# Gated MLP stage of a larger program: another order of block splits, products and weight loads, and two transfers moved from SyncE's queue to GpSimd's

## The chip, the cores and the metric

The program runs on 1 core of one Trainium2 chip. The time is device microseconds of one launch. Three runs of the kernel before took 3770.35, 3770.53 and 3778.82 us, the median is 3770.53 us. The change touches the first of the program's stages alone, the gated MLP mixer, which fills roughly the first 745 us; everything behind it (dilated attention, the second model's mixers, its MLP) is the same code.

## The reference

What the stage computes, with one batch, 1024 tokens, a model width of 1024, 16 heads of 128 features and chunks of 128 tokens:

```
x = residual, h = rms_norm(x, norm_pre[0])
z = h @ w_in                      # 1024 -> 3 x 2048
u, v, g = split(z, 3)
u = gelu(u);  v = layer_norm(gelu(v), vn_g, vn_b)
sg[c, p, head, d] = sum_q w_s[head, p, q] * v[c, q, head, d] + b_s[head, p]
y = u * sg * silu(g)
x = x + rms_norm(y @ w_out, norm_post[0])
```

All of it is float32. The other two mixers and the second MLP of the reference follow on the result x.

## The kernel before, in words

**Precision.** A float32 product is made of three TensorE products: each operand is split into a rounded upper part (ScalarE copies it into a `hi` tile) and a remainder (VectorE subtracts into a `lo` tile), and hi x hi, lo x hi and hi x lo are added up in PSUM. So every operand needs a ScalarE instruction and then a VectorE instruction before TensorE can use it.

**Three parts of the stage.** First the v part: 20 units (`v_units`, five passes of four) multiply h by the weights of v; after each pass ScalarE applies GELU into the staging tile `vst` (two halves, by the feature block f) and VectorE takes `bn_stats` of it; ScalarE's queue stores it to DRAM (`vhat`). Second the heads: for each of 16 heads j, u and g are computed together as a 2x2 block product with seven block products instead of eight (a Winograd form: `Pairs.BLOCKS` are sums of quarters of the weights, `PRODUCTS` names the seven blocks of h they meet: b11, t2, t3, b21, t1, t4, b22, where t1 to t4 are sums of quarters made in place in x by `combine`). Each product is 12 matmuls of 128x512. Then `gating(j)` multiplies the normalised v of that head with w_s (9 float32 matmuls, lines 700 and 702). Third the output: for two token halves and eight column blocks (`outs`), y is multiplied by w_out: `out` with 24 + 24 matmuls (line 740), weights in two buffers `w.raw[0]` and `w.raw[1]`, the lower eight k-tiles from buffer 0 and the upper eight from buffer 1.

**What sets the order.** All queues are written out by hand. Each engine runs its own function in `gmlp`; semaphores tie them. On ScalarE `block_hi(name)` and on VectorE `block_lo(name)` make a block's upper and lower tile (two instructions each), `pairs.split_hi` and `pairs.split_lo` do the same for the seven weight blocks of a head, with four slots. `add_second`, `add_lower`, `add_three`, `add_four` form the weight sums. TensorE waits before product i of a head for `lo_done`, in head 0 also for `s_blo` (the block) and `s_gelu` (the bank is free), and for what VectorE and ScalarE must have read from the bank: `s_c21` before i = 2, `s_x11` before i = 3, `s_c12` before i = 4, `s_n` before i = 5, `s_c22` before i = 6. VectorE's `difference` and the sum into n3 (line 937), and the two sums into `tg` (lines 954 and 960) combine the banks; `gates`, `swish`, `times_value` and `result` make y. The y of the first token half stays in SBUF (`y_of["raw"]`); that of the second half goes to DRAM (`y_rows`) and comes back as `y_late`.

**Tiles that share bytes.** b11 and t2 lie where the early output splits will be; t3 and b21 lie over the upper part of h, t1 and t4 over its lower part, so those four can be written only when the v part no longer reads what is under them. `vst` half 0 shares bytes with gu, tg, th and sv, half 1 with b22. `y_late` and later the residual x again (`x_kept`) lie over the lower part of h.

**Queues.** SyncE's queue issues the weight loads (`w.load` line 132, `pairs.load` lines 230 and 231), v, w_s and b_s of a head (`load_head`, lines 392 to 395), the stores of y (lines 434, 443), the loads of `y_late` (line 449) and one load of 4 MB that brings x back (line 456). GpSimd's queue (lines 1003 to 1016) makes the attention bias tables. Each waits in its written order.

Of the kernel before, what the change touches and what calls it, by code (L numbers as in the profile page):

```python
# [21 lines left out]
P = 128  # L22
# [257 lines left out]
def gmlp(nc, a, w, hi, lo, x_kept, inv, vhat, y_dram, vecs, tiles, ident, ones, yo, norms, blocks, y_of, over_w):  # L280
# [8 lines left out]
    with Stage(nc, "ag") as st:  # L289
# [45 lines left out]
        s_late, s_yhi, s_ylo = (st.sem(n) for n in ("late_in", "yhi_s", "ylo_s"))  # L335
# [18 lines left out]
        made = ("b11", "t2", "t3", "b21", "t1", "t4", "b22")  # L354
# [25 lines left out]
        def _(sp):  # L380
# [82 lines left out]
        def _(act):  # L463
# [45 lines left out]
            for u in range(3, NV):  # L509
# [51 lines left out]
            def y_upper(n):  # L561
# [5 lines left out]
                else:  # L567
                    act.wait_ge(s_late, 16 * (k // 4) + 16)
# [7 lines left out]
            block_hi("t3")  # L576
            for j in range(H):
                last = j == H - 1
                pairs.split_hi(act, j, 3)
                if j == 0:  # L580
                    block_hi("b21")
                    first_product(j)
                    nc.scalar.preload_act_table_set(SQRT_SET)
                    act.wait_ge(s_mv, 1)
                    nc.scalar.activation(sd[:, :], mv[:, :, 1:2].rearrange("p m a -> p (m a)"), ACT.Sqrt, bias=eps[:, :]).then_inc(s_sd, 1)
                    nc.scalar.preload_act_table_set(GELU_SET)
                    block_hi("t1")
                else:
                    value_late(j - 1)
# [3078 lines left out]
```

## Time and profile before

| | us |
|---|---|
| median of 3 runs | 3770.53 |
| profiled execution, its own time | 3774.28 |
| its span, first to last instruction | 3772.7 |
| TensorE busy | 3606.6 (96%) |
| VectorE busy | 1972.8 (52%) |
| ScalarE busy | 1313.0 (35%) |
| mean granted TensorE clock | 0.974 of full speed |

TensorE is busy 96% of the span, so time is lost or won where it stands still or runs at the lower clock. A row of the timeline gives start, duration, engine, line, operation, tiles, count, and in brackets the idle time just ahead and who ended it. Neighbouring instructions overlap at their ends: two 0.69 us operations on VectorE take 1.29 us together.

### The profile page before, as it was taken

The page shows a single profiled execution, that of the slowest core. Times are in us where ns is not written, and L with a number is a line of the kernel's source. Part 1 is how long each engine was busy: PE and PEld are TensorE (multiplying, and loading weights), DVE is VectorE, ACT ScalarE, POOL GpSimd, SP SyncE. Part 2 cuts the span into 40 slices and gives each one's busy share as a digit, 9 for nine tenths or more (in the row PEclk, how much of TensorE's full clock was granted, in tenths as well). Part 3 has the DMA queues.
Part 4 walks back from the last instruction along what each step waited for, and adds up shares of the span by engine and source line. Part 5 has one row for each costly group of instructions (what it writes and reads, how often), then busy time and mean ns, then how long its engine had stood idle before and what let it go on. Part 6 is the DMA issues. An engine that isn't in the chain of part 4 may idle for free. (4 is left out here: it accounts for less than half of the span.)

```text
span 3772.7 us, 48650 instructions
## 1 busy us (share of the span) xinstructions
PE 3606.6 (96%) x18034; PEld 2917.4 (77%) x18034; DVE 1972.8 (52%) x3847; ACT 1313.0 (35%) x2559; POOL 112.2 (3%) x137
## 2 busy tenths in 40 slices
PE   8999999989999999999998899999978999999999
PEld 6878877767777777777777687677977877887887
DVE  5377773263333455555555544544675567654443
ACT  3254443232323333332332434444323323233222
POOL 0000001000000000000000110000000000000000
PEclk9999999999999999999999999999988999999999
DMA  4222335321111111211111330111322322233333
GB/s 146 90 100 85 104 110 164 134 93 59 58 53 52 60 58 61 59 54 46 46 45 50 115 110 19 48 43 63 103 89 95 105 78 84 75 113 95 95 97 121
DMA packets 140772, 308.87 MB, mean 82 GB/s; under 512 B 31824, under 2 KB 70272, under 8 KB 140464
## 3 DMA queue, kind: packets, MB, share of 16 engines
q1 hardware_dynamic: 123792, 264.81, 21.6%
q0 software_dynamic: 14688, 33.22, 2.9%
q10 hardware_dynamic: 2112, 8.39, 0.6%
q8 instruction: 119, 1.95, 0.2%
q14 instruction: 61, 0.50, 0.0%
HBM read 256.55 MB, written 56.04 MB: 83 GB/s over the span
## 5 line engine op out<-in xcount | busy, mean ns | idle before, releaser
L142 DVE TENSOR_TENSOR all_w_lo<-all_w_raw,all_w_hi 128x1024 fp32r<-128x1024 f32 x295 | 361.2, 1225 | 353.5 <-ACT all_w_hi L137 353.3
L137 ACT ACTIVATE all_w_hi<-all_w_raw 128x1024 fp32r<-128x1024 f32 x295 | 310.3, 1053 | 499.2 <-PE om_z L155 261.4
L1433 PE MATMUL da_z<-all_hi,all_w_hi 128*128 128x512 f32 x736 | 306.3, 416 | 4.1 <-DVE all_w_lo L142 4.1
L1433 PE MATMUL da_z<-all_hi,all_w_lo 128*128 128x512 f32 x736 | 291.6, 396 | 0.0
L1433 PE MATMUL da_z<-all_lo,all_w_hi 128*128 128x512 f32 x736 | 290.0, 394 | 0.0
L1294 ACT ACTIVATE da_pt<-da_tr 128x512 f32<-128x512 f32 (+1 forms) x192 | 101.0, 526 | 486.0 <-PE da_tr L1486 486.0
L155 PE MATMUL om_z<-all_hi,all_w_hi 128*128 128x512 f32 x640 | 258.4, 404 | 7.4 <-DVE all_w_lo L142 4.3
L1302 ACT ACTIVATE at_p<-at_logit,da_pair_max 128x256 f32<-128x256 f32 (+1 forms) x384 | 177.9, 465 | 239.6 <-DVE da_pair_max L1688 239.2
L155 PE MATMUL om_z<-all_hi,all_w_lo 128*128 128x512 f32 x640 | 256.3, 401 | 0.0
L155 PE MATMUL om_z<-all_lo,all_w_hi 128*128 128x512 f32 x640 | 254.6, 398 | 0.0
L155 PE MATMUL pr_g<-all_hi,all_w_hi 128*128 128x344 f32 (+1 forms) x624 | 212.7, 341 | 10.6 <-issue 4.9
L155 PE MATMUL pr_g<-all_hi,all_w_lo 128*128 128x344 f32 (+1 forms) x624 | 204.2, 327 | 0.0
L155 PE MATMUL om_z<-om_h_hi,all_w_hi 128*128 128x512 f32 x512 | 202.4, 395 | 1.7 <-DVE all_w_lo L142 1.7
L155 PE MATMUL pr_g<-all_lo,all_w_hi 128*128 128x344 f32 (+1 forms) x624 | 203.2, 326 | 0.0
L155 PE MATMUL om_z<-om_h_hi,all_w_lo 128*128 128x512 f32 x512 | 200.1, 391 | 0.0
L155 PE MATMUL om_z<-om_h_lo,all_w_hi 128*128 128x512 f32 x512 | 200.1, 391 | 0.0
L1688 DVE CUSTOM_DVE_ANT_0 at_logit<-da_qk,at_bias 128x256 f32<-128x256 f32 (+1 forms) x384 | 129.9, 375 | 119.2 <-issue 115.4
L1433 PEld LDWEIGHTS da_z<-all_hi,all_w_hi 128*128 128x128 f32 x736 | 139.0, 189 | 42.0 <-issue 10.6
L1497 PE MATMUL da_pv<-at_v,da_pt 128*128 128x64 f32 x1280 | 164.0, 267 | 0.0
L1433 PEld LDWEIGHTS da_z<-all_lo,all_w_hi 128*128 128x128 f32 x736 | 138.9, 189 | 31.6
L1497 PEld LDWEIGHTS da_pv<-at_v,da_pt 128*128 128x128 f32 x1280 | 159.8, 192 | 2.1
L1433 PEld LDWEIGHTS da_z<-all_hi,all_w_lo 128*128 128x128 f32 x736 | 139.3, 189 | 25.0
(692 smaller groups left out, 7808.5 us busy)
## 6 DMA issues: line engine op xcount, KB each, us to landing
all_w_raw<-in_w_mlp SPq DMA_DIRECT2D x128, 512.0 KB, 3.5
all_w_raw<-in_w_ug SPq DMA_DIRECT2D x48, 512.0 KB, 3.9
all_w_raw<-in_w_qkv SPq DMA_DIRECT2D x48, 512.0 KB, 3.6
all_w_raw<-in_w_in SPq DMA_DIRECT2D x27, 512.0 KB, 3.5
da_w_raw<-in_w_qkv SPq DMA_DIRECT2D x24, 512.0 KB, 3.6
all_w_raw<-in_w_bo SPq DMA_DIRECT2D x24, 512.0 KB, 3.4
all_w_raw<-in_w_v SPq DMA_DIRECT2D x20, 512.0 KB, 4.7
vhat<-ag_vst ACTq DMA_DIRECT2D x4, 2048.0 KB, 7.4
```

Of the source, the lines that this page charges most:

```text
L137: self.nc.scalar.activation(self.hi[b][:, :], self.raw[b][:, :], ACT.Copy).then_inc(self.hi_done[b], 1)
L142: self.nc.vector.tensor_tensor(self.lo[b][:, :], self.raw[b][:, :], self.hi[b][:, :].bitcast(F32), ALU.subtract).then_inc(self.lo_done[b], 1)
L155: last = self.nc.tensor.matmul(out, wp[b][:, w], ap[:, k, cols], start=(k == 0 and m == 0), stop=(k == KT - 1 and m == 2))
L1294: nc.scalar.activation(pt[t % 2][:, 0:wd], tr[t % 2][:, 0:wd], ACT.Copy).then_inc(s_pt, 1)
L1302: last = nc.scalar.activation(p[t % 2][:, hh, 0:wd], logit[t % 2][:, hh, 0:wd], ACT.Exp, scale=-1.0, bias=pair_max[:, t, hh:hh + 1], accum ...
L1433: last = nc.tensor.matmul(z[h][:, :], wp[u][:, ws], ap[:, kk, cols], start=(kk == 0 and m == 0), stop=(kk == KT - 1 and m == 2))
L1497: last = nc.tensor.matmul(pv[t % 2][:, 64 * hh:64 * hh + 64], pt[t % 2][:, i * P:i * P + P], v[:, t + x, 64 * hh:64 * hh + 64], start=(x = ...
L1688: last = nc.vector.tensor_tensor_reduce(out=logit[t % 2][:, hh, 0:wd], in0=qk[hh][:, 0:wd], in1=bias[ag][hh][x][:, :], scale=1.0, scalar=3 ...
```

## The change

Six edits, all in `gmlp`:

1. The tiles change places: b22 now shares bytes with `vst` half 0, gu to sv with half 1. b22 is split already in unit 17 of the v part.
2. The blocks t3, b21 and t1 are split on ScalarE, and t3 and t1 on VectorE, in unit 19, ahead of the GELUs of the last pass; t4 and b21's lower part right after. The sums t1 and t4 are formed there too.
3. VectorE's `bn_stats` of the last pass, and the mean and variance behind it, stand after the products' first sums in head 0, and head 0's weight split 6 and its `tg` sum (`gate_late`) behind them.
4. `gating(j)` stands behind the first product of head j + 1 instead of behind the last of head j.
5. On SyncE's queue the first two pairs of output weights are issued ahead of the head 15 loads, the next two ahead of the last y store; the `y_late` loads leave that queue.
6. GpSimd's queue issues the four `y_late` loads (a semaphore each) and, after the bias tables, x in eight transfers of 512 KB. The y splits 9 to 12 come one output block later.

```diff
         with Stage(nc, "al") as late:
+            blocks["b22"] = tuple(late.sb(f"b22_{part}", [P, KT // 2, HALF], F32R) for part in ("hi", "lo"))
             gu, tg, th, sv = (late.sb(n, [P, T]) for n in ("gu", "tg", "th", "sv"))
-            blocks["b22"] = tuple(late.sb(f"b22_{part}", [P, KT // 2, HALF], F32R) for part in ("hi", "lo"))
...
-        made = ("b11", "t2", "t3", "b21", "t1", "t4", "b22")
+        made_hi = ("b11", "t2", "b22", "t3", "b21", "t1", "t4")
+        made_lo = ("b11", "t2", "b22", "t3", "t1", "b21", "t4")
...
+            def store_y(j):
+                sp.wait_ge(s_y, j + 1)
+                sp.dma_start(y_dram[j], th[:, second_half]).then_inc(s_yout, 16)
+
             for j in range(H):
                 if j == 7:
                     for b in range(2):
                         sp.wait_ge(s_vst[b], 32)
+                if j == H - 1:
+                    sp.wait_ge(pairs.lo_done, Pairs.N * (H - 1))
+                    for b in range(2):
+                        load_out(b, 0)
                 if j:
                     load_head(j)
-                    sp.wait_ge(s_y, j)
-                    sp.dma_start(y_dram[j - 1], th[:, second_half]).then_inc(s_yout, 16)
+                    store_y(j - 1)
                 if j + 2 < H:
                     load_pair(j + 2)
-            sp.wait_ge(pairs.lo_done, Pairs.N * (H - 1))
             for b in range(2):
-                load_out(b, 0)
-            for g in range(4):
-                if g == 3:
-                    sp.wait_ge(s_y, H)
-                    sp.dma_start(y_dram[H - 1], th[:, second_half]).then_inc(s_yout, 16)
-                sp.wait_ge(s_yout, 16 * (4 * g + 4))
-                if g == 0:
-                    sp.wait_ge(pairs.multiplied, Pairs.N * (H - 1) + 6)
-                if g == 3:
-                    load_out(0, 1)
-                sp.dma_start(y_of["late"][:, 4 * g:4 * g + 4, :], y_dram[4 * g:4 * g + 4].rearrange("j p t -> p j t")).then_inc(s_late, 16)
-            load_out(1, 1)
+                load_out(b, 1)
+            store_y(H - 1)
             for n in range(2, NO):
                 for b in range(2):
                     load_out(b, n)
-                if n == KT + 1:
-                    sp.wait_ge(s_ylo, len(splits))
-                    sp.dma_start(x_kept[:, :, :], a["x"]).then_inc(s_xin, 16)
             for b in range(2):
                 w.load(sp, b, n_all, a["w_qkv"][b])
-            sp.wait_ge(s_xin, 16)
+            sp.wait_ge(s_xin, 16 * KT)
             sp.wait_ge(s_norms, 16 * len(norms))
...
+                    if name == "b22":
+                        act.wait_ge(s_vst[0], 32)
+                        act.wait_ge(s_bn, 8 * 3)
...
+                if u == 17:
+                    block_hi("b22")
                 if u == NV - 1:
-                    for i in range(3):
-                        pairs.split_hi(act, 0, i)
+                    pairs.split_hi(act, 0, 0)
+                    w.left(act, 0, v_pairs)
+                    block_hi("t3")
+                    pairs.split_hi(act, 0, 1)
+                    pairs.split_hi(act, 0, 2)
+                    block_hi("b21")
+                    block_hi("t1")
+                    pairs.split_hi(act, 0, 3)
                 if u % 4 == 3:
                     geluses(v_units[u][3])
...
                 if j == 0:
-                    act.wait_ge(s_vst[0], 32)
+                    act.wait_ge(s_vst[1], 32)
+                    act.wait_ge(s_bn, 8 * 4)
...
+            block_hi("t4")
+            first_product(0)
+            for i in range(4, 7):
+                pairs.split_hi(act, 0, i)
+            value(0)
+            nc.scalar.preload_act_table_set(SQRT_SET)
+            act.wait_ge(s_mv, 1)
+            nc.scalar.activation(sd[:, :], mv[:, :, 1:2].rearrange("p m a -> p (m a)"), ACT.Sqrt, bias=eps[:, :]).then_inc(s_sd, 1)
+            nc.scalar.preload_act_table_set(GELU_SET)
+            pairs.split_hi(act, 1, 0)
+            act.wait_ge(s_shift, 1)
+            normalise(0)
+            for i in range(1, 3):
+                pairs.split_hi(act, 1, i)
...
                     last.then_inc(pairs.multiplied, 1)
-                gating(j)
+                    if i == 0 and j:
+                        gating(j - 1)
+            gating(H - 1)
...
+                if u == 17:
+                    block_lo("b22")
                 if u == NV - 1:
                     w.left(dve, 0, v_pairs)
                     pairs.add_second(dve, 0)
                     pairs.add_lower(dve, 0)
                     pairs.split_lo(dve, 0, 0)
+                    block_lo("t3")
                     pairs.add_three(dve, 0)
                     pairs.split_lo(dve, 0, 1)
+                    dve.wait_ge(s_sums, 4)
+                    dve.wait_ge(s_blo, 8)
+                    combine("t1", "t2", "b22", ALU.subtract)
                     pairs.split_lo(dve, 0, 2)
-                if u % 4 == 3:
+                    block_lo("t1")
+                    dve.wait_ge(s_sums, 6)
+                    combine("t4", "t2", "b21", ALU.subtract)
+                    pairs.split_lo(dve, 0, 3)
+                    pairs.add_four(dve, 0)
+                elif u % 4 == 3:
                     statistics(v_units[u][3])
-            block_lo("t3")
-            dve.wait_ge(s_bn, 8 * 4)
-            for m in range(KT):
-                last = nc.vector.bn_aggr(mv[:, m, :], stats[:, 4 * m:4 * m + 4, :])
-            last.then_inc(s_mv, 1)
+            w.left(dve, 1, v_pairs)
+            block_lo("b21")
...
+            pairs.split_lo(dve, 0, 4)
+            block_lo("t4")
+            difference(0)
+            pairs.split_lo(dve, 0, 5)
+            sum_of_three(0)
+            statistics(len(passes) - 1)
+            dve.wait_ge(s_bn, 8 * 4)
+            for m in range(KT):
+                last = nc.vector.bn_aggr(mv[:, m, :], stats[:, 4 * m:4 * m + 4, :])
+            last.then_inc(s_mv, 1)
+            pairs.split_lo(dve, 0, 6)
+            dve.wait_ge(s_vst[1], 32)
+            gate_late(0)
+            dve.wait_ge(s_sd, 1)
+            nc.vector.reciprocal(rstd[:, :], sd[:, :]).then_inc(s_rstd, 1)
+            dve.wait_ge(s_rstd, 1)
+            nc.vector.scalar_tensor_tensor(shift[:, :], mv[:, :, 0:1].rearrange("p m a -> p (m a)"), -1.0,
+                                           rstd[:, :], ALU.mult, ALU.mult).then_inc(s_shift, 1)
+            pairs.add_second(dve, 1)
+            pairs.add_lower(dve, 1)
+            pairs.split_lo(dve, 1, 0)
+            gate_early(0)
+            pairs.add_three(dve, 1)
+            pairs.split_lo(dve, 1, 1)
+            pairs.split_lo(dve, 1, 2)
...
+            pool.wait_ge(pairs.multiplied, Pairs.N * (H - 1) + 6)
+            for g in range(4):
+                pool.wait_ge(s_yout, 16 * (4 * g + 4))
+                pool.dma_start(y_of["late"][:, 4 * g:4 * g + 4, :], y_dram[4 * g:4 * g + 4].rearrange("j p t -> p j t")).then_inc(s_late[g], 16)
             pool.dma_start(hot, a["hot"]).then_inc(s_bin_v, 16)
...
             pool.wait_ge(s_bout, 48 + 16 * 12)
+            pool.wait_ge(s_ylo, len(splits))
+            for k in range(KT):
+                pool.dma_start(x_kept[:, k, :], a["x"][:, k, :]).then_inc(s_xin, 16)
```

How rows stand now. VectorE, from head 0's weight split 3 on (`p_lo` is the lower part of a weight block in one of four slots; ba, bb, al are where a block's tiles lie; `all_yo` is x; `all_inv` is n2 or n3). Before:

```order
L267 TENSOR_TENSOR ag_p_lo3<-all_w_raw0,ag_p_hi3 128x512 [waits ag_p_hi_done,ag_lnp_in]
L251 TENSOR_TENSOR all_w_raw0<-all_w_raw0 128x512 [waits ag_p_summed]
L805 TENSOR_TENSOR ba_b21_lo<-all_yo,ba_b21_hi 128x1024 [waits ag_block_hi] x2
L879 TENSOR_TENSOR all_inv<-all_inv,ag_bank1 128x512 [waits ag_x11_s,ag_p_multiplied]
L810 TENSOR_TENSOR all_yo<-all_yo 128x2x512 [waits ag_block_lo,ag_sums_s]
L810 TENSOR_TENSOR all_yo<-all_yo 128x2x512
L805 TENSOR_TENSOR bb_t1_lo<-all_yo,bb_t1_hi 128x1024 [waits ag_block_hi] x2
L810 TENSOR_TENSOR all_yo<-all_yo 128x2x512 [waits ag_sums_s]
L810 TENSOR_TENSOR all_yo<-all_yo 128x2x512
L267 TENSOR_TENSOR ag_p_lo0<-ow_spare,ag_p_hi0 128x512 [waits ag_p_hi_done]
```

The same engine now, from head 0's weight split 3 to the sum that TensorE needs before product 6:

```order
L267 TENSOR_TENSOR ag_p_lo3<-all_w_raw0,ag_p_hi3 128x512 [waits ag_p_hi_done]
L251 TENSOR_TENSOR all_w_raw0<-all_w_raw0 128x512 [waits ag_p_summed]
L808 TENSOR_TENSOR ba_b21_lo<-all_yo,ba_b21_hi 128x1024 [waits ag_block_hi,all_w_multiplied1]
L808 TENSOR_TENSOR ba_b21_lo<-all_yo,ba_b21_hi 128x1024 [waits ag_block_hi]
L267 TENSOR_TENSOR ag_p_lo0<-ow_spare,ag_p_hi0 128x512 [waits ag_p_hi_done,ag_lnp_in]
L808 TENSOR_TENSOR bb_t4_lo<-all_yo,bb_t4_hi 128x1024 [waits ag_block_hi] x2
L890 TENSOR_TENSOR all_inv<-all_inv,ag_bank1 128x512 [waits ag_x11_s,ag_p_multiplied]
L267 TENSOR_TENSOR ag_p_lo1<-all_w_raw1,ag_p_hi1 128x512 [waits ag_p_hi_done]
L920 TENSOR_TENSOR all_inv<-ag_bank2,all_inv 128x512 [waits ag_n_s,ag_p_multiplied]
L799 BN_STATS ag_stats<-ag_vst 128x6 [waits ag_gelu_s] x8
L939 BN_AGGR ag_mv<-ag_stats 128x2 [waits ag_bn_s]
```

The two `combine` sums and t1's lower part, which stood in this piece, are now ahead of it; the eight `bn_stats` and the `bn_aggr`, which stood ahead of it, are now in it, and weight split 6 (`ag_p_lo2`) and the sum `al_tg` come after them.

SyncE's queue from the loads of head 15 on (`ow_v`, `all_ident` and `ag_bs` are v, w_s and b_s of the head; `all_w_raw` the output weights). Before:

```order
L392 DMA ow_v<-vhat 128x1024 [waits ag_sg_s]
L393 DMA all_ident<-in_ws_t 128x128
L395 DMA ag_bs<-in_b_s 128x128 [waits ag_s_read]
L434 DMA y_rows<-al_th 128x512 [waits ag_y_s]
L132 DMA all_w_raw0<-in_w_ug 128x1024 [waits all_w_lo_done0,ag_p_lo_done]
L132 DMA all_w_raw1<-in_w_ug 128x1024 [waits all_w_lo_done1]
L449 DMA y_late<-y_rows 128x4x512 [waits ag_p_multiplied,ag_y_stored]
L449 DMA y_late<-y_rows 128x4x512 [waits ag_y_stored] x2
L443 DMA y_rows<-al_th 128x512 [waits ag_y_s]
L132 DMA all_w_raw0<-in_w_ug 128x1024 [waits all_w_lo_done0,ag_y_stored]
```

The same queue now:

```order
L132 DMA all_w_raw0<-in_w_ug 128x1024 [waits all_w_lo_done0,ag_p_lo_done]
L132 DMA all_w_raw1<-in_w_ug 128x1024 [waits all_w_lo_done1]
L394 DMA ow_v<-vhat 128x1024 [waits ag_sg_s]
L395 DMA all_ident<-in_ws_t 128x128
L397 DMA ag_bs<-in_b_s 128x128 [waits ag_s_read]
L431 DMA y_rows<-al_th 128x512 [waits ag_y_s]
L132 DMA all_w_raw0<-in_w_ug 128x1024 [waits all_w_lo_done0]
L132 DMA all_w_raw1<-in_w_ug 128x1024 [waits all_w_lo_done1]
L431 DMA y_rows<-al_th 128x512 [waits ag_y_s]
```

The first output weights no longer stand behind a store of y, the second pair no longer behind the last store and the `y_late` transfers.

## Rows read from the trace of the kernel before

**Rows 1.** Who TensorE waited for, 535 to 600 us: total, times, longest

```profile
PE ag_bank L740 <- issue: 8.0, 2, 5.3
```

**Rows 2.** The same view, 650 to 760 us

```profile
PE ag_bank L740 <- issue: 3.7, 1, 3.7
```

**Rows 3.** TensorE's timeline, head 0 to the start of head 1

```profile
198.92 0.39 PE L275 MATMUL ag_bank<-ag_b_hi,ag_p_hi 128*128 128x512 f32 x1
...
209.79 0.39 PE L275 MATMUL ag_bank<-ba_b_lo,ag_p_hi 128*128 128x512 f32 x1
217.48 0.80 PE L275 MATMUL ag_bank<-bb_t_hi,ag_p_hi 128*128 128x512 f32 x1 [7.30 <-DVE ag_p_lo L267]
...
223.52 0.39 PE L275 MATMUL ag_bank<-bb_t_lo,ag_p_hi 128*128 128x512 f32 x1
...
227.91 0.47 PE L275 MATMUL ag_bank<-al_b_hi,ag_p_hi 128*128 128x512 f32 x1 [1.95 <-issue]
...
232.68 0.48 PE L275 MATMUL ag_bank<-ag_b_hi,ag_p_hi 128*128 128x512 f32 x1
```

**Rows 4.** ScalarE's timeline: the last pass's first two GELUs, one block's upper part

```profile
194.44 1.29 ACT L485 ACTIVATE ag_vst<-ag_bank,ag_inv_col 128x512 f32<-128x512 f32 x2 [2.60 <-PE ag_bank L680]
...
200.31 2.01 ACT L495 ACTIVATE ba_t_hi<-all_yo 128x1024 fp32r<-128x1024 f32 x2 [0.50 <-ACT ag_vst L485]
```

**Rows 5.** VectorE's timeline: weight sum, statistics, one block's lower part

```profile
188.16 0.69 DVE L236 TENSOR_TENSOR ow_spare<-all_w_raw 128x512 f32<-128x512 f32 x1 [8.79 <-PE ag_bank L680]
...
195.16 1.29 DVE L796 BATCH_NORM_STATS2 ag_stats<-ag_vst 128x6 f32<-128x512 f32 x2 [2.51 <-ACT ag_vst L485]
...
201.40 2.36 DVE L805 TENSOR_TENSOR ba_t_lo<-all_yo,ba_t_hi 128x1024 fp32r<-128x1024 f32 x2 [0.86 <-ACT ba_t_hi L495]
203.68 1.11 DVE L858 BATCH_NORM_AGGREGATE ag_mv<-ag_stats 128x2 f32<-128x24 f32 x8
```

**Rows 6.** TensorE's timeline, the first two output blocks

```profile
552.53 0.47 PE L740 MATMUL ag_bank<-ye_hi,all_w_hi 128*128 128x512 f32 x1 [2.73 <-issue]
...
568.28 0.77 PE L740 MATMUL ag_bank<-ye_hi,all_w_hi 128*128 128x512 f32 x1 [5.31 <-issue]
...
578.75 0.80 PE L740 MATMUL ag_bank<-ym_hi,all_w_hi 128*128 128x512 f32 x1 [2.53 <-DVE all_w_lo L142]
...
581.86 0.39 PE L740 MATMUL ag_bank<-ym_hi,all_w_lo 128*128 128x512 f32 x1
```

**Rows 7.** VectorE's timeline and SyncE's queue, the same stretch

```profile
546.37 3.49 DVE L904 TENSOR_TENSOR ym_lo<-y_raw,ym_hi 128x1024 fp32r<-128x1024 f32 x3
551.20 1.23 DVE L142 TENSOR_TENSOR all_w_lo<-all_w_raw,all_w_hi 128x1024 fp32r<-128x1024 f32 x1 [1.35 <-ACT all_w_hi L137]
...
560.22 0.33 SPq L443 DMA_DIRECT2D y_rows<-al_th  x1
562.21 0.35 SPq L132 DMA_DIRECT2D all_w_raw<-in_w_ug  x1
```

**Rows 8.** SyncE's queue and ScalarE around the load of x

```profile
634.20 0.33 SPq L132 DMA_DIRECT2D all_w_raw<-in_w_ug  x1
656.57 0.67 SPq L456 DMA_DIRECT2D x_kept<-in_x  x1
661.40 0.34 SPq L132 DMA_DIRECT2D all_w_raw<-in_w_ug  x1
...
643.25 1.06 ACT L137 ACTIVATE all_w_hi<-all_w_raw 128x1024 fp32r<-128x1024 f32 x1 [4.96 <-DMA all_w_raw<-in_w_ug]
678.13 1.06 ACT L137 ACTIVATE all_w_hi<-all_w_raw 128x1024 fp32r<-128x1024 f32 x1 [9.71 <-DMA all_w_raw<-in_w_ug]
```

**Rows 9.** Landing of the 16 loads of v; head 3's sum ahead of product 6

```profile
DMA to landing us min/median/max: 3.1/3.3/4.3
289.76 0.69 DVE L954 TENSOR_TENSOR al_tg<-ag_bank,all_inv 128x512 f32<-128x512 f32 x1
291.23 0.39 PE L275 MATMUL ag_bank<-al_b_hi,ag_p_hi 128*128 128x512 f32 x1
```

More of the change, by code:

```diff
@@ L334, in gmlp @@
         s_x11, s_n, s_c11, s_c12, s_c21, s_c22, s_gu = (st.sem(n) for n in ("x11_s", "n_s", "c11_s", "c12_s", "c21_s", "c22_s", "gu_s"))
-        s_late, s_yhi, s_ylo = (st.sem(n) for n in ("late_in", "yhi_s", "ylo_s"))
+        s_late = st.sems("late_in", 4)
+        s_yhi, s_ylo = (st.sem(n) for n in ("yhi_s", "ylo_s"))
         block = st.block()
@@ L575, in _ @@
             w.left(act, 1, v_pairs)
-            block_hi("t3")
-            for j in range(H):
+            block_hi("t4")
[12 more added lines that the diff above has]
+                pairs.split_hi(act, 1, i)
+            for j in range(1, H):
                 last = j == H - 1
                 pairs.split_hi(act, j, 3)
[L580 to L589, printed above, removed]
-                    first_product(j)
+                value_late(j - 1)
+                first_product(j)
                 pairs.split_hi(act, j, 4)
-                if j:
-                    gate(j - 1)
-                if j == 0:
-                    block_hi("t4")
+                gate(j - 1)
                 pairs.split_hi(act, j, 5)
-                if j == 0:
-                    act.wait_ge(s_vst[1], 32)
-                    block_hi("b22")
-                    act.wait_ge(s_shift, 1)
-                if j:
-                    normalise(j)
+                normalise(j)
                 pairs.split_hi(act, j, 6)
-                if j == 0:
-                    normalise(j)
                 if last:
@@ L632, in _ @@
                 w.split_hi(act, 0, v_pairs + n + 1)
-                if n in (2, 3, 4, 5):
-                    y_upper(9 + n - 2)
+                if n in (3, 4, 5, 6):
+                    y_upper(9 + n - 3)
                 if n == KT - 1:
@@ L904, in y_lower, with sum_of_three @@
                 nc.vector.tensor_tensor(y_lo, raw, y_hi.bitcast(F32), ALU.subtract).then_inc(s_ylo, 1)
-            for j in range(H):
-                last = j == H - 1
-                if j:
-                    last_value(j - 1)
-                pairs.split_lo(dve, j, 3)
-                pairs.add_four(dve, j)
-                if j == 0:
-                    block_lo("b21")
-                    difference(j)
-                    dve.wait_ge(s_sums, 4)
-                    dve.wait_ge(s_blo, 6)
-                    combine("t1", "t2", "b22", ALU.subtract)
-                    block_lo("t1")
-                    dve.wait_ge(s_sums, 6)
-                    combine("t4", "t2", "b21", ALU.subtract)
-                pairs.split_lo(dve, j, 4)
-                if j:
-                    gates(j - 1)
-                    difference(j)
-                else:
-                    dve.wait_ge(s_sd, 1)
-                    nc.vector.reciprocal(rstd[:, :], sd[:, :]).then_inc(s_rstd, 1)
-                    dve.wait_ge(s_rstd, 1)
-                    nc.vector.scalar_tensor_tensor(shift[:, :], mv[:, :, 0:1].rearrange("p m a -> p (m a)"), -1.0,
-                                                   rstd[:, :], ALU.mult, ALU.mult).then_inc(s_shift, 1)
-                    block_lo("t4")
-                pairs.split_lo(dve, j, 5)
-                if j:
-                    swish(j - 1)
+            def sum_of_three(j):
                 done(Pairs.N * j + 3)
@@ L937, in _, with gate_late, gate_early @@
                 nc.vector.tensor_tensor(n3, bz, n2, ALU.add).then_inc(s_n, 1)
-                if j == 0:
-                    block_lo("b22")
+            def gate_late(j):
+                done(Pairs.N * j + 5)
+                dve.wait_ge(s_n, 2 * j + 2)
+                nc.vector.tensor_tensor(tg[:, second_half], bw, n3, ALU.add).then_inc(s_c22, 1)
+            def gate_early(j):
+                done(Pairs.N * j + 6)
+                nc.vector.tensor_tensor(tg[:, first_half], bz, n2, ALU.add).then_inc(s_c21, 1)
+            pairs.split_lo(dve, 0, 4)
[23 more added lines that the diff above has]
+            pairs.split_lo(dve, 1, 2)
+            for j in range(1, H):
+                last = j == H - 1
+                last_value(j - 1)
+                pairs.split_lo(dve, j, 3)
+                pairs.add_four(dve, j)
+                pairs.split_lo(dve, j, 4)
+                gates(j - 1)
+                difference(j)
+                pairs.split_lo(dve, j, 5)
+                swish(j - 1)
+                sum_of_three(j)
                 pairs.split_lo(dve, j, 6)
@@ L942, in _ @@
                     pairs.add_second(dve, j + 1)
-                if j:
-                    times_value(j - 1)
+                times_value(j - 1)
                 if not last:
@@ L951, in _ @@
                         y_lower(n)
-                done(Pairs.N * j + 5)
-                dve.wait_ge(s_n, 2 * j + 2)
-                nc.vector.tensor_tensor(tg[:, second_half], bw, n3, ALU.add).then_inc(s_c22, 1)
+                gate_late(j)
                 if not last:
                     pairs.split_lo(dve, j + 1, 1)
-                if j:
-                    result(j - 1)
-                done(Pairs.N * j + 6)
-                nc.vector.tensor_tensor(tg[:, first_half], bz, n2, ALU.add).then_inc(s_c21, 1)
+                result(j - 1)
+                gate_early(j)
                 if not last:
```

11 lines of the change are left out of this document (5 added, 6 removed).

## The prediction

> **What bounds the kernel now.** I read the page first, then who TensorE waited for, stretch by stretch, then the timelines of the queues around each place. The page gives TensorE 96% busy, so a change of order can only win where it stands or runs at the low clock. Within the stage that is touched there are three such places, and the reader is to see in each who comes last.
>
> *Place A, head 0.* TensorE starts head 0 at 198.92 and does four products without a stop until 209.79 [rows 3]: 48 matmuls, so 0.227 us from one to the next and 2.72 us a product. Then it stands 7.30 us for VectorE, and 1.95 us more before product 6. VectorE is behind since it works through statistics, six block halves and two sums in that time. After the 7.30 us the matmuls run at the lower of the two clock levels: 14 of them from 217.48 to 223.52 take 6.04 us where 3.17 would do, 2.9 us lost [rows 3].
>
> *Place B, the first two output blocks.* TensorE waits 2.73, 5.31 and 2.53 us [rows 6]; the first two are 8.0 us "issue", which is a load that came late [rows 1]: the second output weight is issued at 562.21, since SyncE's queue held it behind the last y store at 560.22 [rows 7]. Eight matmuls from 578.75 to 581.86 take 3.11 us where 1.81 would do [rows 6], so a short drop of the clock costs 1.3 us; I take the same for the start at 568.28, which has the same long first matmul. The waits of 1.95 and 2.73 us are followed by a first matmul of 0.47 us, at the full clock [rows 3, 6].
>
> *Place C, the load of x.* SyncE's queue issues 4 MB at 656.57; the weight load issued behind it at 661.40 is used at 678.13, 16.7 us later [rows 8], and TensorE stands 3.7 us [rows 2]. With one short clock drop that is 5.0 us.
>
> All else in the stage (15 heads, 14 output blocks) runs with TensorE busy without a break.
>
> **The change part by part.**
>
> *Place A, what comes instead.* VectorE's pace is 0.60 us for a 128x512 operation (two statistics take 1.29, of which the last's end overlaps) and 1.14 for half a block [rows 5]. From 188.2, when unit 18 lets it begin, to the sum `al_tg` that product 6 of head 0 waits for, the new order holds 14 operations of 128x512 (8.5 us), six pairs of halves (12 x 1.14 = 13.7), eight statistics (4.8) and the aggregation (1.1): 28.1 us, to 216.3. It also waits for ScalarE: 0.8 at weight split 1 (needs a VectorE sum, then ScalarE), 0.6 at t1 (the same), 1.7 at split 4, which ScalarE can do only after eight GELUs at 0.60 and t4's upper part at 2.0 [rows 4], and 0.1 for the result. Together 219.5.
>
> ScalarE: t3 from 188.2, splits 1 and 2 after the sum at 193.0, b21 to 196.0, t1 after its sum from 196.7 to 198.6, split 3 to 199.15, first GELU read out at 199.85. Product 0 needs that bank, so head 0 starts at 199.87, 0.95 us later than before. The later GELUs are done at 0.60 each while a product lasts 2.72, so they cost nothing. Products 3, 4 and 5 (b21 at 205.9, t1 at 200.1, t4 at 210.5, n3 at 212.3) are ready ahead of their turns at 208.1, 210.8 and 213.5. Product 6 would be due at 216.2 and gets `al_tg` at 219.5: a new wait of 3.3 us. A wait of 3.3 lies between 2.53 and 5.31, which both brought the short drop, so 1.3 us for the clock. Behind it the mean, the standard deviation and `normalise(0)` end near 224.3; `gating(0)`, now behind head 1's first product, is due after 226, so they are covered, which is what moving it buys.
>
> Place A: 7.30 + 1.95 + 2.9 gone, 0.95 + 3.3 + 1.3 new: 6.6 us gained. Bounds: with statistics as slow as 0.68 us each (they may have been paced by something else before) and a long clock loss 2.9, only 4.3; with no drop 7.9.
>
> *b22 in unit 17* lies beside a v unit in which VectorE and ScalarE are mostly idle: nothing. If the store it waits for were late, it still has 40 us.
>
> *Gating behind the next first product, heads 1 to 15.* The same work, so no direct gain. But v's load is issued when the gating is done, now 4.7 us into the head, and lands 3.3 us later [rows 9], where before it lay ready. Queued behind it on ScalarE are `normalise`, weight split 6, then `value`; on VectorE split 6, `times_value`, three more operations and `al_tg`, which product 6 waits for. Counted from a head's start: v at 8.2, normalised 11.3, split 6 at 12.6, `times_value` 14.4, `value` and the next head's split 0 on ScalarE 15.6, its lower part 16.3, `add_three` 16.9, `al_tg` 17.5. Product 6 is due at 6 x 2.72 + 1.93 = 18.3. Margin 0.8 us; before it was 291.23 - 290.45, also 0.8 [rows 9]. So nothing, but with the slowest landing of v (4.3) the margin is gone.
>
> *Place B.* The first output weights are issued in head 14's wake, so VectorE can split the first right after the y splits, at 549.8 instead of 551.20 [rows 7]: 1.5 us. From that split to the last y store it took 9.0 us (551.20 to 560.22); the same chain ends at 558.8 now. ScalarE's last y split 0.5, weight split 1.1 and VectorE's 1.2 follow, and no longer a load, which is issued at 551.0 and has 8 us: output block 1 can start at 561.7, while block 0 ends at 561.5 (it took 10.45). So 568.28 becomes 561.7: 6.6 us, and the clock drop of 1.3 goes with the wait. The 2.53 us wait behind it is ScalarE and VectorE splitting a weight that may be written only after block 0 ends; unchanged, with its drop. Place B: 7.8 us; bounds 6.3 (the y loads that now run beside the weight load make it 9 us late, as one was: issued 634.20, used 643.25 [rows 8]) and 9.1.
>
> *Place C.* x no longer stands ahead of a weight load, so 5.0 us go. What is late next: 4 MB run beside weight loads instead of ahead of one. While GpSimd's bias tables moved, a load took 9.05 us and TensorE did not stop [rows 8], so a doubled landing is covered. Bounds: 5.0 gained, and 5.0 lost if two loads come later still. I take 5.0, the row of 9.05 being nearest.
>
> By the Trainium skill, DMA: Bandwidth & Descriptors, section "Queues, rings and completion order", each DMA engine goes round between queue rows, a packet from each. The trace bears it out as far as it goes: 16.7 us behind x on one queue against 9.05 beside another queue's tables. By that rule a weight load gets every second packet while x runs and takes about 1.4 us more; with the queue as the trace shows it, the sum stands as it is.
>
> *`y_late` and x on GpSimd's queue* are needed some 45 and 60 us after their issue: nothing.
>
> **Sum.** 6.6 + 7.8 + 5.0 = 19.4 us. The profiled execution took 3774.28, so 3754.9; the median of the runs is 3.75 below it, so 3751 us.
>
> **Rivals.**
> 1. *x only changes its queue, not its cost.* The 16 engines moved at full rate through x's load; weight loads late by 3 us or more would leave place C as it is. For: GpSimd issues eight transfers within few us. Against: the 9.05 us load. Gain 14.4: 3756.
> 2. *The new wait in head 0 is as long as the old.* VectorE's chain has no slack and 26 links; 3 us more of waits for ScalarE, with a long clock loss, take all of place A. Gain 12.8: 3758.
> 3. *The heads lose a little.* If v lands at 4.3 to 4.8 us, each of 15 heads waits 0.2 to 0.7 us, 7 us on average. Gain 12: 3759; a third of this case is slower than 3759.2 and within the bound.
> 4. *The heads lose much: slower.* One mechanism, the chain v, `normalise`, split 6, `al_tg`. It decides from 19.4 / 15 = 1.3 us a head, that is v landing 2.1 us later than 3.3. If it lands at 6.8, 2.7 us a head: 40 lost, 19 gained, 3791. Against: at that time in a head nothing but 64 KB of w_s is in flight.
> 5. *The change does not do what it says*, b22 or the sums coming late for another reason; half the gain: 3761.
>
> **How the numbers follow.** Forecast 0.60, rival 1 0.13, rival 2 0.08, rival 3 0.10, rival 4 0.04, rival 5 0.05. The forecast's own range is 3747 to 3755. Rivals 1 to 3 end within 3760, and bounds of both signs (place C's 5.0, place B's 1.3, place A's 1.3) reach from 3746 up; the range is 3745 to 3761, which leaves out rivals 4 and half of 5. A measurement tells 0.3%, 11.3 us, from no change, so faster is below 3759.2: forecast, rivals 1 and 2 but a part, and two thirds of rival 3 give 0.86; same 0.10; slower 0.04.
>
> **What would show it.** In the changed profile: the 7.3 us wait gone, and one wait of about 3.3 us before the `al_b_hi` product, ended by VectorE's `al_tg`; product 0 0.95 us later than the v part's end; heads still 21.07 us apart without a wait; `al_tg` some 0.8 us before product 6; output blocks 0 and 1 without a wait over 1.5 us, then one of 2.5; no wait of TensorE after that until the stage ends. The forecast fails if a wait shows up inside the heads 1 to 14, or a weight load lands more than 9 us after its issue while x moves.

## The result, and the profile after

The changed kernel takes 3748.2 us (median of 4 runs, 3746.1 to 3754.0), the kernel before beside it 3772.0: ratio 0.9937 with a 95% interval of 0.9922 to 0.9951. Forecast were 3751 us and a range of 3745 to 3761. The profiled executions have spans of 3772.7 and 3744.9 us. Cut at the points at which the prediction spoke:

| TensorE, from ... to ... | before | changed | gain | forecast |
|---|---|---|---|---|
| span's start to the v part's last matmul | 198.7 | 199.3 | -0.6 | 0 |
| place A: to product 6 of head 15 | 346.1 | 339.3 | 6.8 | 6.6 |
| place B: to the upper half of output block 1 | 34.0 | 25.9 | 8.0 | 7.8 |
| place C: to the stage's last matmuls | 171.2 | 165.9 | 5.3 | 5.0 |
| the later stages (no edit) | 3022.7 | 3014.5 | 8.3 | 0 |

"Stage length" below is the sum of A, B and C, 551.3 us before and 531.1 changed: a gain of 20.1 where 19.4 were forecast.

Who TensorE waited for in the changed kernel, first 190 to 250 us, then 535 to 600 us (total, times, longest):

```profile
PE ag_bank L275 <- DVE ag_p_lo L267: 2.9, 1, 2.9
PE ag_bank L275 <- issue: 0.7, 1, 0.7
...
PE ag_bank L743 <- DVE all_w_lo L142: 2.5, 1, 2.5
PE ag_bank L743 <- issue: 1.6, 2, 1.3
PE ag_bank L275 <- DVE al_tg L925: 0.7, 1, 0.7
```

A wait "<- issue" has no releaser in the profile. The 7.30 and 1.95 us of [rows 3] have become 0.7 and 2.9, the 2.73 and 5.31 of [rows 6] 1.3 and 0.3, and the 3.7 of [rows 2] has no successor. TensorE's timeline around the new wait:

```profile
199.28 0.39 PE L681 MATMUL ag_bank<-all_w_hi,all_lo 128*128 128x512 f32 x1
200.42 0.47 PE L275 MATMUL ag_bank<-ag_b_hi,ag_p_hi 128*128 128x512 f32 x1 [0.74 <-issue]
...
219.89 0.68 PE L275 MATMUL ag_bank<-al_b_hi,ag_p_hi 128*128 128x512 f32 x1 [2.89 <-DVE ag_p_lo L267]
220.37 0.63 PE L275 MATMUL ag_bank<-al_b_hi,ag_p_lo 128*128 128x512 f32 x1
...
224.31 0.39 PE L275 MATMUL ag_bank<-ag_b_hi,ag_p_hi 128*128 128x512 f32 x1
...
227.06 0.39 PE L701 MATMUL ag_bank<-all_ident,all_ones 128*128 128x128 f32 x2
```

The twelve matmuls from 219.89 to 224.31 take 4.42 us instead of 2.72: the low clock costs 1.7. VectorE's timeline says who was really last, since a wait for several semaphores bears one name only:

```profile
207.99 0.69 DVE L267 TENSOR_TENSOR ag_p_lo<-ow_spare,ag_p_hi 128x512 fp32r<-128x512 f32 x1 [1.56 <-ACT ag_p_hi L262]
...
212.67 4.83 DVE L799 BATCH_NORM_STATS2 ag_stats<-ag_vst 128x6 f32<-128x512 f32 x8
217.53 1.12 DVE L939 BATCH_NORM_AGGREGATE ag_mv<-ag_stats 128x2 f32<-128x24 f32 x8
218.57 0.63 DVE L267 TENSOR_TENSOR ag_p_lo<-all_w_raw,ag_p_hi 128x512 fp32r<-128x512 f32 x1
219.11 0.68 DVE L925 TENSOR_TENSOR al_tg<-ag_bank,all_inv 128x512 f32<-128x512 f32 x1
```

`al_tg` ends at 219.79, 0.1 us before product 6; the 1.56 us that VectorE stands for weight split 4 is the 1.7 that the prediction named. In heads 1 to 14 nothing waits. The same sum and product 6 in head 3, and the first matmuls of product 6 in head 15 and of the output (TensorE and VectorE):

```profile
283.35 0.69 DVE L925 TENSOR_TENSOR al_tg<-ag_bank,all_inv 128x512 f32<-128x512 f32 x1
284.81 0.39 PE L275 MATMUL ag_bank<-al_b_hi,ag_p_hi 128*128 128x512 f32 x1
...
537.52 0.39 PE L275 MATMUL ag_bank<-bb_t_lo,ag_p_hi 128*128 128x512 f32 x1
538.61 0.47 PE L275 MATMUL ag_bank<-al_b_hi,ag_p_hi 128*128 128x512 f32 x1 [0.70 <-DVE al_tg L925]
538.92 0.40 PE L275 MATMUL ag_bank<-al_b_hi,ag_p_lo 128*128 128x512 f32 x1
...
544.90 0.47 PE L743 MATMUL ag_bank<-ye_hi,all_w_hi 128*128 128x512 f32 x1 [1.29 <-issue]
555.61 0.47 PE L743 MATMUL ag_bank<-ye_hi,all_w_hi 128*128 128x512 f32 x1 [0.26 <-issue]
```

In head 3 the margin is 284.81 - 284.04 = 0.8 us, as in [rows 9]. It isn't so in every head: in head 4 v landed after 3.9 us, and `al_tg`, started at 305.07, ended 0.15 us before product 6 at 305.90.

```profile
305.07 0.68 DVE L925 TENSOR_TENSOR al_tg<-ag_bank,all_inv 128x512 f32<-128x512 f32 x1
305.90 0.47 PE L275 MATMUL ag_bank<-al_b_hi,ag_p_hi 128*128 128x512 f32 x1
```

### The profile page after: what moved, and what is told of

Same layout as the page of the kernel before. It is cut to its first block and busy times, and to the rows that moved or that the text cites. A ratio compares the mean times of both kernels' runs of the same rounds, so it can differ in the third digit from the quotient of the medians.

```text
span 3744.9 us, 48660 instructions
## 1 busy us (share of the span) xinstructions
PE 3593.3 (96%) x18034; PEld 2908.0 (78%) x18034; DVE 1977.8 (53%) x3847; ACT 1313.2 (35%) x2559; POOL 119.7 (3%) x149
## 3 DMA queue, kind: packets, MB, share of 16 engines
q8 instruction: 119, 1.95, 0.2%
```

## The experiments

Each is read by its stage length, from one trace; the totals stand beside it. The changed kernel's own two traces give 531.1 and 530.9 us, and one low-clock stretch is worth 1.5 to 1.7 us, so a difference below that is read from the single waits.

**The queue edits alone.** SyncE's and GpSimd's programs of the changed kernel on the kernel before. What goes ahead of head 15's loads is one pair of weight loads (both halves for output block 0), not two pairs as edit 5 has it, and one pair more goes ahead of the last y store.

```diff
+                if j == H - 1:
+                    sp.wait_ge(pairs.lo_done, Pairs.N * (H - 1))
+                    for b in range(2):
+                        load_out(b, 0)
...
+            for k in range(KT):
+                pool.dma_start(x_kept[:, k, :], a["x"][:, k, :]).then_inc(s_xin, 16)
```

> The kernel before with edits 5 and 6 alone (SyncE's and GpSimd's queues, the y splits one block later); head 0 and the gating stay as before. Theory, three places that add up: the 7.3 and 1.95 us waits in head 0 stay, the waits after head 15 shrink to those of the changed kernel, no wait after 600 us; the last matmuls of the stage, which start behind the 1.3 us wait (749.96 before, 730.41 changed), start 8.0 + 5.3 = 13.3 us earlier, at 736.7. Rival, the queue edits pay only with the new order of the heads in front of them: gain under 8 us, 742 or later.

Measured: stage length 537.9, 13.3 less than before; place A unchanged with its 7.3 us wait, B 25.9 and C 165.9 us long as in the changed kernel. Total 3754.4 us (4 runs), ratio 0.9958 [0.9941, 0.9974]. Places B and C don't need the new heads.

**The heads alone.** The changed kernel with these edits undone.

```diff
-                load_out(b, 1)
-            store_y(H - 1)
+                load_out(b, 0)
+            for g in range(4):
+                if g == 3:
+                    sp.wait_ge(s_y, H)
+                    sp.dma_start(y_dram[H - 1], th[:, second_half]).then_inc(s_yout, 16)
...
```

> The changed kernel with edits 5 and 6 undone: its head 0 and gating, the old queues. Theory: one wait of 2.9 us in head 0, after head 15 the old waits of about 2.8, 5 and 2.5 us, and 3.7 us behind the load of x; the stage's last matmuls start 6.8 us earlier than before, at 743.1. Rival, the parts depend on one another: the two gains alone don't sum to the 19.5 us of both, off by more than 2 us.

Measured: stage length 546.6, only 4.7 less than before where 6.8 were expected; total 3761.1 us (7 runs), ratio 0.9975 [0.9963, 0.9988]. Place A gained 7.2, but B was 1.4 and C 1.1 us longer than before. Its waits after head 15 and behind x, and the clock in 535 to 580 us, then the same 45 us of the kernel before, in which product 6 of head 15 starts 8.9 us later (columns: us, busy time of each engine with instructions, granted clock, DMA share, GB/s):

```profile
PE ag_bank L749 <- issue: 11.2, 3, 4.6
PE ag_bank L749 <- DVE all_w_lo L142: 2.5, 1, 2.5
535.00:580.00 45.00, 35.23 (x136) 27.88 (x135) 19.39 (x24) 12.36 (x15) 1.67 (x3) 0.85 0.59 192
544.00:589.00 45.00, 33.83 (x142) 27.27 (x142) 20.94 (x25) 12.86 (x16) 1.66 (x3) 0.92 0.59 192
```

The 11.2 us are 2.9, 3.7 and 4.6. In B the waits are 1.4 us less than before, but the clock takes that back and more: 0.85 over these 45 us, where the kernel before has 0.92. In C the wait behind x is 0.9 longer. The two gains sum to 18.0 against 20.1 together. The rival's bound of 2 us is passed by 0.1, in one trace each: what differs in B is the clock behind the waits, and whether it falls so in every execution no run shows.

**Queue or size of the x transfer.** Two versions of the changed kernel. Eight transfers on SyncE:

```diff
+                if n == KT + 1:
+                    sp.wait_ge(s_ylo, len(splits))
+                    for k in range(KT):
+                        sp.dma_start(x_kept[:, k, :], a["x"][:, k, :]).then_inc(s_xin, 16)
...
-            for k in range(KT):
-                pool.dma_start(x_kept[:, k, :], a["x"][:, k, :]).then_inc(s_xin, 16)
```

> The changed kernel with x in eight transfers of 512 KB, but issued one behind the other on SyncE's queue where the one transfer of 4 MB stood. If it is the queue that held up the weight load behind x, TensorE waits 3 to 4.5 us once after 640 us and the clock drops, 5 us lost: last matmuls near 735.5. If it was the size of the single transfer, no wait and 730.4.

One transfer on GpSimd:

```diff
-            for k in range(KT):
-                pool.dma_start(x_kept[:, k, :], a["x"][:, k, :]).then_inc(s_xin, 16)
+            pool.dma_start(x_kept[:, :, :], a["x"]).then_inc(s_xin, 16)
```

> The changed kernel with x as one transfer of 4 MB on GpSimd's queue. If it is the queue, no wait of TensorE after 600 us and the last matmuls at 730.4, weight loads landing within 8 us. If the size counts, a wait of about 3.7 us comes back and they start near 735.5.

Measured: 537.8 and 531.4. On SyncE TensorE waits once behind x, and the matmuls after it run at the low clock. The wait is 5.0 us where 3 to 4.5 were expected, and the stage is 6.7 us longer, not 5. The weight load issued behind x lands late (TensorE's timeline, then the landing of that load, then of the first load issued while x moves in the changed kernel):

```profile
667.11 0.77 PE L747 MATMUL ag_bank<-ao_y_hi,all_w_hi 128*128 128x512 f32 x1 [5.01 <-issue]
667.68 0.63 PE L747 MATMUL ag_bank<-ao_y_hi,all_w_lo 128*128 128x512 f32 x1
```

```profile
DMA to landing us min/median/max: 17.2/17.2/17.2
```

```profile
DMA to landing us min/median/max: 7.2/7.2/7.2
```

With one 4 MB transfer on GpSimd the first weight load beside x lands after 7.5 us and x after 15.9 (8 transfers: 11.5), with no wait of TensorE. Slower loads stand in both traces (8.0 us in the changed kernel, 9.0 in this one), but they were issued at 642.5 and 640.1, ahead of x and beside the bias tables. So it is the queue, not the size. On SyncE x is issued at 641.7, on GpSimd only at 657.2, behind the tables; but the moment is not what counts, for on SyncE the load issued at 641.4, just ahead of x, landed after 7.7 us and the one behind x after 17.2. Rival 1 of the prediction falls. By the Trainium skill, DMA: Bandwidth & Descriptors, section "Queues, rings and completion order", a DMA engine serves its queue rows by turns, a packet from each: the traces agree in that a load beside x on another row isn't held to x's end (7.2 and 6.8 us for the first two, 17.2 behind x on one row). The 1.4 us more that the prediction put beside it was too little: against a landing of 3.4 they take 3.4 to 3.8 more.

**Gating at the head's end.**

```diff
-                    if i == 0 and j:
-                        gating(j - 1)
-            gating(H - 1)
+                gating(j)
```

> The changed kernel with gating(j) behind the last product of head j again, for every head; the rest as changed. Counted from the v part's last matmul to the stage's last matmuls (531.1 us in the changed kernel). Theory, the move covers normalise(0), done at 224.85, and nothing else: TensorE waits 0.3 to 0.6 us for it at the end of head 0, heads 1 to 14 show no wait, 531.5. Rival, the early gating costs the heads margin: the 0.7 us wait in head 15 goes and the stage becomes shorter, under 531.

Measured: 531.6, one new wait of 0.42 us, ended by `normalise(0)`; the wait in head 15 stayed at 0.6. In the changed kernel the early gating thus buys half a microsecond. It also costs what the rival names, though without a wait: here v landed after up to 4.2 us and `al_tg` still ended 0.8 us ahead of product 6 in each of heads 1 to 14, where the changed kernel has 0.15 in head 4.

**Gating one product later.**

```diff
-                    if i == 0 and j:
+                    if i == 1 and j:
```

> The changed kernel with gating(j) behind the second product of head j + 1 instead of the first, 2.72 us later. Theory, the chain of gating, load of v, normalise, weight split 6 and al_tg has 0.8 us of margin: it is now short by about 1.9 us in each of heads 1 to 15, TensorE waits 1.7 to 2.0 us before product 6 each time, and the 531.1 us become 558 to 562. Rival, the chain has slack or isn't the one that decides: under 535.

Measured: stage length 571.0, total 3788.6. The waits of heads 1 to 14, and TensorE's timeline at one of them:

```profile
PE ag_bank L275 <- DVE al_tg L925: 27.2, 14, 2.3
```

```profile
288.90 0.47 PE L275 MATMUL ag_bank<-al_b_hi,ag_p_hi 128*128 128x512 f32 x1 [1.94 <-DVE al_tg L925]
289.20 0.51 PE L275 MATMUL ag_bank<-al_b_hi,ag_p_lo 128*128 128x512 f32 x1
289.52 0.63 PE L275 MATMUL ag_bank<-al_b_lo,ag_p_hi 128*128 128x512 f32 x1
```

1.9 us a head, 2.72 less the 0.8 of margin: the chain is shown, and its margin for most heads. The stage length was missed by 9 to 13 us. To the 27.2 come 2.7 more in head 15, some 3.5 for the 14 stops (see the last section), and the low clock behind four of these waits and head 15's, 1.7 each or 8.5; 1.6 go in output block 0, which no longer waits: 40.3, and 39.8 were measured.

**Weight split 4 first.**

```diff
+            pairs.split_hi(act, 0, 4)
             block_hi("t4")
             first_product(0)
-            for i in range(4, 7):
+            for i in range(5, 7):
```

> The changed kernel with one instruction moved on ScalarE: weight split 4 of head 0 ahead of t4's upper part. Theory: VectorE no longer stands 1.56 us for it, al_tg comes that much earlier, and the 2.9 us wait before product 6 becomes 1.3. A wait of this length (0.7, 1.3 and 1.95 us are in the traces) was followed by no low clock, so 1.7 us more: 531.1 becomes 527.9. Rival a, the clock drops all the same: 529.5. Rival b, VectorE's statistics decide whatever stands before them: 531.

Measured: 527.8. TensorE's timeline: 

```profile
215.56 0.47 PE L275 MATMUL ag_bank<-al_b_hi,ag_p_hi 128*128 128x512 f32 x1 [1.24 <-DVE ag_p_lo L267]
215.87 0.39 PE L275 MATMUL ag_bank<-al_b_hi,ag_p_lo 128*128 128x512 f32 x1
```

The wait is 1.24 us and full clock follows it. The new wait of the change was VectorE's pace plus one needless stop of 1.56 us.

**Tile 15 in block 0.**

```diff
-                if n == 1:
-                    out(0, 1, upper[-1:])
                 w.split(pe, 1, v_pairs + n)
-                out(n, 1, upper[:-1] if n == 0 else upper)
+                out(n, 1, upper)
```

> The changed kernel with the last y tile of output block 0 multiplied in its own place, instead of after the first half of block 1. Theory: that tile is split at 553.96, due at 555.1, so TensorE doesn't wait for it; weight buffer 1 is free 5 us earlier and its split is covered, the 2.54 us wait goes with its low clock, the 0.26 us one too: 531.1 becomes 526.6. Rival a, the wait goes and the clock drops elsewhere: 528.3. Rival b, the tile comes late and the wait moves to block 0's end: 531.

Measured: 527.1. The waits of 2.54 and 0.26 are gone with their low clock. In head 0 the low clock behind the wait of 2.87 lasted longer in this trace, 14 matmuls in 6.06 us, and cost 2.9 instead of 1.7; but for that it would be 525.9 (an estimate).

**The first GELU ahead of split 3.**

```diff
+                    if f == 3 and m == ms[0]:
+                        pairs.split_hi(act, 0, 3)
...
-                    pairs.split_hi(act, 0, 3)
```

> The changed kernel with weight split 3 of head 0 behind ScalarE's first GELU instead of ahead of it. Theory, an early wait that isn't the last: the 0.74 us wait before head 0 shrinks to 0.2, and the 2.9 us wait before product 6 grows to 3.4, since VectorE's chain doesn't move: 531.1 stays. Rival: the head starts earlier and stays earlier, 530.6.

Measured: 530.9; the waits are 0.22 and 3.40 where they were 0.74 and 2.89. The length lies between theory and rival and tells nothing, since the changed kernel's second trace has 530.9 too; the waits are those of the theory. Head 0 starts earlier and meets the same `al_tg`.

**Both edits, all edits, and the changed kernel again,** in one series on one chip. Both edits are the two diffs above. All edits add, among others, these moves on VectorE (ScalarE's `pairs.split_hi(act, 1, 0)` moves as well):

```diff
-                    pairs.split_lo(dve, 0, 1)
...
                     combine("t1", "t2", "b22", ALU.subtract)
+                    pairs.split_lo(dve, 0, 1)
...
+            for m in range(KT):
+                last = nc.vector.bn_aggr(mv[:, m, :], stats[:, 4 * m:4 * m + 4, :])
+            last.then_inc(s_mv, 1)
+            pairs.add_second(dve, 1)
+            pairs.add_lower(dve, 1)
+            pairs.split_lo(dve, 1, 0)
...
+            w.split_lo(dve, 0, v_pairs)
             for n in range(4, 7):
                 y_lower(n)
-            w.split_lo(dve, 0, v_pairs)
```

> The changed kernel with the two measured single edits together: split 4 ahead of t4, tile 15 in block 0. Theory, they lie in different places and add up: 531.1 - 3.3 - 4.0 = 523.8 to 523.3 us from the v part to the stage's last matmuls, 7 to 8 us less in all. Rival: with one of them the other's clock drop comes back, 525.5.

> The changed kernel with the waits that are left reordered away: split 4 first and tile 15 in block 0 as measured alone, and in head 0 t1's sum ahead of weight split 1, the mean and variance behind the al_tg sum, head 1's first split ahead of the square root; behind head 15 the output weight's lower part ahead of three y splits, al_tg ahead of the fourth y split, y split 7 behind the last y. Theory: VectorE's pace decides in both places, so its standing still goes and waits of 0.3, 0.6, 0.8, 0.6 and 0.8 us are left, all too short for the low clock: 531.1 us from the v part to the stage's last matmuls becomes 520.6, and the kernel takes 10 us less than the changed one. Rival, more than two of the moves only hand their wait on: 523 to 524, as for two edits.

> The changed kernel once more, beside the others: 531.1 us from the v part to the stage's last matmuls, as in its first trace; 3748 to 3753 us in all. Theory: the part behind the stage, which no edit touches, differs from run to run by the low-clock stretches in it, so that the 4 us between the stage's gain (20.1) and the difference of the medians (23.8) are scatter. Rival: the later stages are faster behind the changed stage by some 4 us or more: 3748 again, and the same shorter remainder.

| 5 runs each | stage length | median us | ratio to before, 95% |
|---|---|---|---|
| changed again | 530.9 | 3749.6 | 0.9944 [0.9930, 0.9957] |
| two edits | 522.8 | 3742.5 | 0.9922 [0.9908, 0.9935] |
| all reordered | 521.1 | 3739.7 | 0.9914 [0.9900, 0.9927] |

The two edits save 8.4 us together, 0.6 to 1.1 more than forecast: with both in place no low clock is left anywhere in the stage, where tile 15 alone still had the long one of 2.9 us in head 0. All of them leave waits of 0.6 us and less, to be read in who TensorE waited for from 190 to 700 us:

```profile
PE ag_bank L744 <- issue: 0.6, 1, 0.6
PE ag_bank L702 <- ACT ow_v L541: 0.5, 1, 0.5
PE ag_bank L744 <- DVE ym_lo L914: 0.3, 1, 0.3
PE ag_bank L275 <- issue: 0.3, 1, 0.3
```

It is the fastest version: 9.9 us below the changed kernel in the same series, 32.5 below the kernel before. The moves beyond the two edits bring 1.7 us of stage length: the waits of the two edits, 0.74, 1.21, 0.61 and 1.27 us, become the four above, 2.1 us less in sum. Which of the moves did it no run tells.

**The later stages.** No edit touches them, and each trace has the same 14834 matmuls there. They last 3022.7 us before and 3014.5 changed, but in the other traces 3013.9 (all reordered) to 3025.8 us (x on SyncE), 3016.8 for the changed kernel again. One row of each, before, changed and two edits (first column the stretch from the stage's last matmuls on):

```profile
749.96:3772.70 3022.74, 2895.22 (x14834) 2332.56 (x14834) 1553.86 (x3304) 1006.52 (x2079) 95.91 (x115) 0.97 0.23 73
```

```profile
730.41:3744.90 3014.49, 2886.64 (x14834) 2326.13 (x14834) 1554.22 (x3304) 1006.69 (x2079) 96.08 (x115) 0.98 0.23 73
```

```profile
719.83:3743.40 3023.57, 2902.78 (x14834) 2338.48 (x14834) 1553.83 (x3304) 1006.59 (x2079) 95.87 (x115) 0.97 0.23 73
```

Two edits have a faster stage in front still and yet the longer remainder of before. TensorE's busy time for the same matmuls is 16.1 us longer there than in the changed kernel, so its clock was lower, and 7.1 us less idle time gives a part of it back. Of the 27.8 us between the spans, 8.3 lie in the later stages, 20.1 in this one, and 0.6 were lost before it. That the 8.3 are scatter is borne out by the two edits' trace, but a small gain behind the stage isn't excluded. The medians' 22.7 and 23.8 against 20.1 lie within their intervals; yet in all six comparisons the medians differ by more than the stage lengths, by 1.3 to 6.8 us, the most for the heads alone (11.5 against 4.7). Comparisons of one series share their runs of the kernel before, so these are not six independent signs.

## Why the prediction was right

*Place A, product 0.* Forecast 0.95 us late; it waits 0.74, and 1.14 lie between two starts that are else 0.23 apart, so it is 0.9 late. Right, and for the reason given: with the GELU ahead of split 3 the wait shrinks.

*Place A, product 6.* Forecast a wait of 3.3 us for `al_tg`; it is 2.89, for `al_tg`. VectorE's stops for ScalarE were put at 0.8, 0.6 and 1.7 us and are 0.70, 0.53 and 1.56:

```profile
194.22 0.69 DVE L267 TENSOR_TENSOR ag_p_lo<-all_w_raw,ag_p_hi 128x512 fp32r<-128x512 f32 x1 [0.70 <-ACT ag_p_hi L262]
198.31 2.36 DVE L808 TENSOR_TENSOR bb_t_lo<-all_yo,bb_t_hi 128x1024 fp32r<-128x1024 f32 x2 [0.53 <-ACT bb_t_hi L493]
```

That they add to VectorE's own 28.1 us was right too: with the longest taken out, the wait falls by it. The clock was taken at 1.3 and cost 1.7. The 1.3 was a miscount: from 578.75 to 581.86 [rows 6] there are eight starts but seven steps, 1.59 us at full clock, so that drop cost 1.5. That the shorter wait and the dearer clock cancel, 6.6 against 6.8, is luck. So is a part of the clock term itself: of the two waits next to 3.3 us on the short side, 2.53 us brought the drop and 2.73 did not [rows 6], and the prediction took it as certain.

*Gating.* That `normalise(0)` is covered by head 1's first product was right, for 0.4 us. That this chain decides in the heads is shown by the experiment one product later. The 0.8 us of margin hold for most heads only: it is 0.7 to 0.8 us in 11 of heads 1 to 14, 0.5 in two and 0.15 in one. The prediction said why: it goes with v's landing. In the changed trace v's 16 loads landed within 3.9 us and none of heads 1 to 14 waited, so rivals 3 and 4 fall:

```profile
DMA to landing us min/median/max: 3.1/3.3/3.9
```

In two other traces with the early gating one load took 4.3 us, and the head it belongs to waited 0.2 us. This is the one with x in one transfer on GpSimd:

```profile
303.87 0.47 PE L275 MATMUL ag_bank<-al_b_hi,ag_p_hi 128*128 128x512 f32 x1 [0.22 <-DVE al_tg L925]
```

So rival 3's mechanism is real; what was missing is a landing as late in every head.

*Place B.* Output block 0 was forecast 1.5 us earlier after its first weight and waits 1.29 instead of 2.73. Block 1 was put at 561.7 on the old time scale; place A moved it 6.2 earlier, to 555.5, and it starts at 555.61. The wait of 2.53 behind it was forecast unchanged and is 2.54. The queue edits alone give the same 8.0. The prediction's own terms, 6.6 and 1.3, give 7.9 and not 7.8.

*Place C.* Forecast 5.0; 5.3 by the two traces and by the queue edits alone. Putting x back on SyncE in eight pieces costs more, 6.7 us, as its wait is 5.0 and not 3.7 us.

*What was off.* The sum was 0.7 us low for the stage. TensorE's waits in the three places (without the 1.3 us ahead of the stage's last matmuls, which both kernels have) sum to 24.1 us before and 8.4 changed, so 15.7 of the 20.1 us are waits that went; the rest is the low clock, by difference some 4.2, and 0.25 for there being one stop fewer. The two drops that the sum prices at 1.3 us each, behind the waits of 5.31 and 3.7 us, cost 1.6 and 1.7. The median was 2.8 below the forecast; the runs of the same kernel lie 8 to 9 us apart, so that isn't to be explained.

## What to carry to other kernels

Where an engine is 96% busy, cut the trace at its few stops and sum each by who comes last; a gain of 0.5% could so be forecast to within a microsecond at each place, while the ratio of the whole program has an interval of some 0.15% (5.5 us) to each side. A bulk transfer issued ahead of a load that is waited for costs no less in small pieces than in one; on another queue it cost no wait here. Moving a link of a chain later can leave every wait as it is and still use up the margin that covered a late transfer: look at the margin in each head, not in one. Before taking out a wait, look for the next one on the same chain: the early GELU gained nothing, the split that VectorE itself stood for gained all of its 1.56 us and the low clock on top.

## What the hardware showed beside that

A stop costs TensorE more than its idle time: around the idle 0.70 us before 538.61 the next two steps from start to start are 1.09 and 0.31 us, 0.95 us beyond two steps of 0.23, so 0.25 more.

The low clock follows short stops irregularly. Between the v part and the stage's last matmuls every stop of 0.2 to 1.3 us was followed by the full clock in all 14 traces, and all 20 stops of 2.5 and of 2.9 us by the low one within 1.5 us; the 2.73 us of [rows 6] were not, nor were the 1.95 of [rows 3], and of 14 stops of 1.7 to 2.3 us in one kernel four were. So a forecast can price a wait of 1.7 to 2.8 us only with a chance of 1.7 us more; bringing it to 1.3 us or less kept the clock in all traces here.
